# High and low weight halves behind the exponent and the scaled probabilities; unit 7's split a step sooner, one modulation piece a step later

## The reference, cut to what matters

```python
q, k, v, f, z = jnp.split(h @ w_in, SPLIT0, axis=-1)
...
logits = jnp.concatenate([sink_logits(sink, s_win.shape[:-1]), s_ctx, s_win], axis=-1)
p = jax.nn.softmax(logits, axis=-1)
...
y = jnp.concatenate([windowed_attention(q, k, v, kc, vc, sink), fourier_mix(f, w_f)], axis=-1)
x = x + gate[:, None] * ((y * jax.nn.silu(z)) @ w_out)
```

## Time and profile before

| | us |
|---|---|
| median of 3 runs | 1442.05 (1441.32 to 1442.59) |
| profiled execution | 1441.64 |
| its span, first to last instruction | 1440.0 |
| TensorE busy | 1409.8 |
| VectorE busy | 904.3 |
| ScalarE busy | 501.6 |

### The profile page before, as it was taken

The page is one execution under the profiler, slowest core; times in us unless marked ns, Lnnn a source line. Parts: engine busy times, 40 slices in busy tenths (PEclk is TensorE's granted clock), DMA queues, the critical chain, the costliest instruction groups (busy, mean ns, idle before and its releaser), DMA issues.

```text
span 1440.0 us, 20122 instructions
## 1 busy us (share of the span) xinstructions
PE 1409.8 (98%) x7714; PEld 1183.1 (82%) x7714; DVE 904.3 (63%) x1422; ACT 501.6 (35%) x730; POOL 77.1 (5%) x148
## 2 busy tenths in 40 slices
PE   5999999999999999999999999999999999999997
PEld 3788888888888888888888888888888888888897
DVE  6645656456767687776556676664555666674456
ACT  5223322244555344444222342112351323332233
POOL 0001111011100000000010001000000000010000
PEclk9999999999999999999999999999999999999999
DMA  9996667557611333324666656333323232366345
GB/s 384 408 385 223 197 214 255 165 177 217 206 58 54 105 109 115 117 75 158 204 193 191 199 177 205 117 91 100 99 92 102 88 101 90 98 197 191 104 145 174
DMA packets 65099, 236.87 MB, mean 164 GB/s; under 512 B 7232, under 2 KB 8128, under 8 KB 63744
## 3 DMA queue, kind: packets, MB, share of 16 engines
q1 hardware_dynamic: 43344, 157.83, 33.2%
q0 software_dynamic: 19712, 72.03, 16.0%
q10 hardware_dynamic: 1968, 5.95, 1.2%
HBM read 231.59 MB, written 4.19 MB: 164 GB/s over the span
## 4 chain that ended last, share of the span: by engine, by line
PE 93%; DVE 5%; issue 1%; ACT 1%; DMA 0%; DVEq 0%; ACTq 0%
PE ps L1385 91%; PE ps L1613 2%; DVE w_lo L798 1%; DVE kvmem L944 1%; DMA vec<-in_vectors 0%; DVE stat L1065 0%; DVE pooled L1346 0%; DVE kvmem L860 0%; DVE tmp L917 0%; DVE pt_lo L1104 0%; DVE modchunk L805 0%; DVE main L921 0%; DVE tmp L1076 0%; ACT scratch L533 0%; DVE h_lo L870 0%
## 5 line engine op out<-in xcount | busy, mean ns | idle before, releaser
L1385 PE MATMUL ps<-h_hi,w_hi 128*128 128x512 f32 (+1 forms) x1664 | 643.2, 387 | 1.0 <-DVE w_lo L798 0.5
L1385 PE MATMUL ps<-h_hi,w_lo 128*128 128x512 f32 (+1 forms) x1664 | 634.6, 381 | 0.0
L1385 PE MATMUL ps<-h_lo,w_hi 128*128 128x512 f32 (+1 forms) x1664 | 634.2, 381 | 0.0
L798 DVE TENSOR_TENSOR w_lo<-raw,w_hi 128x1024 fp32r<-128x1024 f32 x216 | 264.3, 1224 | 358.4 <-ACT w_hi L437 358.0
L437 ACT CAST w_hi<-raw 128x1024 fp32r<-128x1024 f32 x216 | 226.5, 1049 | 646.1 <-PE ps L1385 646.0
L1385 PEld LDWEIGHTS ps<-h_hi,w_hi 128*128 128x128 f32 x1664 | 312.9, 188 | 63.7 <-issue 5.4
L1385 PEld LDWEIGHTS ps<-h_hi,w_lo 128*128 128x128 f32 x1664 | 312.8, 188 | 61.2
L1385 PEld LDWEIGHTS ps<-h_lo,w_hi 128*128 128x128 f32 x1664 | 313.2, 188 | 56.8 <-issue 0.2
L805 DVE CUSTOM_DVE_ANT_0 modchunk<-modchunk,cond_row 128x1024 f32<-128x1024 f32 x128 | 154.8, 1219 | 21.1 <-DMA modchunk<-in_modb 21.1
L392 POOL DMA_DIRECT2D modchunk<-in_modb x128 | 67.6, 528 | 1140.2 <-DVE modacc L805 1115.8
L641 ACT CAST pt_hi<-ps 128x512 fp32r<-128x512 f32 (+1 forms) x48 | 30.7, 639 | 124.1 <-PE ps L1613 124.1
(11 more groups left out here) (206 smaller groups left out, 1343.5 us busy)
## 6 DMA issues: line engine op xcount, KB each, us to landing
raw<-in_weights SPq DMA_DIRECT2D x216, 512.0 KB, 3.6
modchunk<-in_modb POOLq DMA_DIRECT2D x128, 512.0 KB, 4.6
raw<-in_mod SPq DMA_DIRECT2D x32, 512.0 KB, 8.6
modchunk<-in_mod SPq DMA_DIRECT2D x16, 512.0 KB, 7.2
cond_row<-in_mod SPq DMA_DIRECT2D x16, 512.0 KB, 9.0
main<-in_xT SPq DMA_DIRECT2D x4, 1024.0 KB, 8.9
main<-in_xT ACTq DMA_DIRECT2D x4, 1024.0 KB, 4.9
out<-pooled SPq DMA_DIRECT2D x14, 256.0 KB, 2.1
```

The source lines that it names most:

```text
L798: nc.vector.tensor_tensor(w_lo[:, j % 2], src, w_hi[:, j % 2].bitcast(F32), ALU.subtract).then_inc(lo_ready, 1)
L1385: return nc.tensor.matmul(out, lhsT, rhs, start=start, stop=stop, skip_group_check=True)
```

## The change

Two tables change: the sixth entry of `UNIT_SLOTS` (the split of unit 7, counted from 0, the last of the group) from step 11 to 10, and the fifth of `JOB_SLOTS` from 10 to 11, where now two pieces stand. In a step, `hi` goes from the front of ScalarE's list to behind the exponent, and `lo` from behind the maximum to behind the scaled probabilities, ahead of modulation pieces, tile splits and rotations. In the first pass `hi` stands ahead of the swap. The work is the same.

```diff
-UNIT_SLOTS = (2, 4, 6, 7, 9, 11, 13)
+UNIT_SLOTS = (2, 4, 6, 7, 9, 10, 13)
 QUERY_SLOTS = (2, 5, 8)
-JOB_SLOTS = (1, 3, 5, 8, 10, 11, 12)
+JOB_SLOTS = (1, 3, 5, 8, 11, 11, 12)
...
-                    if k in UNIT_SLOTS:
-                        s = UNIT_SLOTS.index(k)
-                        hi(i + G_Z, s + 2)
                     if k in QUERY_SLOTS:
...
                     if k < STEPS and (k or first):
                         exponent(i, k)
+                    if k in UNIT_SLOTS:
+                        s = UNIT_SLOTS.index(k)
+                        hi(i + G_Z, s + 2)
...
-                    if k in UNIT_SLOTS:
-                        s = UNIT_SLOTS.index(k)
-                        if s < HALVES - 2 or last:
-                            lo(i + G_Z, s + 2)
                     if k in QUERY_SLOTS:
...
                     if k < STEPS and (k or first):
                         probabilities(i, k)
-                    if k in JOB_SLOTS and not (first or last):
-                        job(i + (M_Z - 1), JOB_SLOTS.index(k))
+                    if k in UNIT_SLOTS:
+                        s = UNIT_SLOTS.index(k)
+                        if s < HALVES - 2 or last:
+                            lo(i + G_Z, s + 2)
+                    for j, slot in enumerate(JOB_SLOTS):
+                        if slot == k and not (first or last):
+                            job(i + (M_Z - 1), j)
```

## The result

The changed kernel takes 1448.91 us, the median of 6 runs (1448.12 to 1450.13), against 1441.9 for the kernel before in the same comparison: 7.0 us more, a ratio of 1.0047 with a 95% interval of 1.0037 to 1.0058. The forecast was 1448.6 us. The profiled execution took 1448.12 us with a span of 1446.4, 6.4 above the span before; it is the shortest of the six.

The account below looks back on a forecast made before the run. TensorE was taken to bound the kernel, but VectorE the ends of passes two and three. Chunk waits 6.8, gains 0.35 and 0.4, loss 0.5 made +6.5 us on 1442.05: 1448.6 us, 8-in-10 range 1445.9 to 1452.0.

Parts of the forecast that it names:

- The bound and the place: End of passes two and three: VectorE, not TensorE, sets the time, with 0.05 us of slack.
- The chain to the late chunk: Passes two and three: late fifth piece delays the seventh chunk's load; seventh piece 3.4 us late each time, 6.8 us.
- L: Time from POOL's issue of the seventh chunk's load to its landing, taken as 4.3 us (3.9 to 5.6).
- Step 11 of the first pass: Probabilities come sooner for the transposes of step 12: gain 0.35 us (0 to 0.8).
- Step 3 of the third pass: Scores no longer held by a query piece behind the low half at step 2: gain 0.4 us.
- Step 11 of the second and third pass: Waits of 0.2 to 0.25 us for probabilities vanish, but gain nothing at the pass end.
- The last pass: Step 10 gets the low half ahead of the tile splits, delaying step 11's probabilities: loss 0.5 us (0 to 0.9).
- The fit of step 4: Unit split at step 4 is ready for step 5's first filler with 0.35 us to spare; costed at nothing.
- A: Rival at the ends of passes two and three: the chunk's load is hidden after all; 1441.5 us, chance 7%.
- B: Rival across the attention stage: transposes gain at every step, excess of about 4 us goes; 1438 us, chance 2%.
- C: Rival: units also come late, step 4's 0.35 us missing, and paired DMA takes 5 to 5.6 us; 1452 us, chance 12%.
- D: Rival at the seventh chunk: POOL can't prepare the load while VectorE works, 1.3 us later; 1451.2 us, chance 7%.

Follow-up runs that it names:

- piece_7_late: The full change with the seventh modulation piece moved from step 12 to step 13; 1442.58 us, ratio 0.9998 to the kernel before.
- split_parts: The full change except that the fifth modulation piece stays at step 10; 1443.61 us, ratio 1.0010 to the kernel before.

## Why the prediction was right, point by point

**The bound and the place.** That VectorE sets the time at the end of passes two and three held: the low half came 2.99 us later and TensorE's filler 2.99 us later. The rows that made the point were the earlier trace rows, three engines across one pass end. The first engine to feel the delay was another than I had named: TensorE waited for the output of the last block (line 1084) and not for the query piece; both are queued behind the seventh piece, so the amount is the same. So the sign that I had given, a wait of about 3 us for the low half, was seen in two parts: 2.0 us for the block's output and 0.3 and 1.0 for the low half.

**The chain to the late chunk.** Fifth piece forecast at 522.5, measured 522.53; issue forecast 524.4, measured 524.41; seventh piece forecast 528.7, measured 528.27. The step that failed is L, the landing: its size, not the chain. I took 4.3 us because another load follows at once. The landing of the load at 524.41:

```profile
DMA to landing us min/median/max: 3.8/3.8/3.8
```

The second load didn't slow the first here; it took longer itself, 4.6 us from its own issue at 525.56. The row of 4.3 us that I took as nearest shared its time with a load issued ahead of it: SP had issued a weight load in the kernel before at 522.28, and that one landed only 4.3 us later. In the changed kernel the weight load is issued at 520.18 and takes 3.5 us, so it has landed before 524.41. The 3.9 of a load alone was the row to take. That doesn't hold for every pair: at 299 and 310 us of the changed kernel, with a weight load in flight at the first issue, both loads of a pair took 5.1 to 5.5 us. The term was 6.8 us and should have been 6.0.

**What was missing.** The sum had no term for TensorE's clock. A wait of 2 us on TensorE wasn't over here when it ended: products behind it ran at 1.2 GHz for some microseconds. In the profiled run of the change that is 0.8 us, all at the fourth pass; at the third it is given back by step 2. With the measured sizes the sum is 6.0 + 0.8 - 0.4 - 0.5 + 0.2 = 6.1, for the 6.0 us of lag gained in the stage. The total came out close by luck: the clock's 0.8 us, which I had left out, stand for the 0.8 by which L was too large. The other runs of the change point the same way: the two longest, 1450.1 us, have a mean granted clock of 0.993, the profiled one of 1448.12 us has 0.995. The median is 0.8 us above the profiled run; that the clock makes this too is likely by these means, but not shown.

**The gains.** Step 11 of the first pass: forecast 0.35 us; the wait at the transposes of step 12 fell from 0.64 to 0.20, and over the pass 0.36 us were won. Step 3 of the third pass: forecast 0.4, measured 0.44 to 0.54; the query piece ends before TensorE needs it. Step 11 of the second and third pass: the 0.25 us were won there, and as forecast they gave nothing at the end of the second pass, since VectorE decides there.

**The losses.** The last pass: forecast 0.5 us, measured 0.2. The transposes of step 12 still wait, as the row of the changed kernel shows:

```profile
676.16 0.66 PE L1614 MATMUL ps<-kvmem,tmp 128*128 128x128 f32 x4 [0.27 <-DVE tmp L1076]
```

The maximum of step 11 came as late as forecast: at 673.69 against 666.49, 1.0 us beyond the lag of 6.2. But the scaling of the probabilities came only 0.2 us late beyond that lag (675.62 against 669.20), because the low half no longer stood between the two; I had put it at 0.5.

The fit of step 4, which I had costed at nothing with 0.35 us to spare: in the changed kernel's second pass the low half starts at 485.01 and the filler at 486.72, without a wait.

```profile
485.01 1.23 DVE L798 TENSOR_TENSOR w_lo<-raw,w_hi 128x1024 fp32r<-128x1024 f32 x1 [0.19 <-ACT w_hi L437]
...
486.72 0.47 PE L1386 MATMUL ps<-h_hi,w_hi 128*128 128x512 f32 x1
```

**The rivals.** A and B fall with the two waits for chunks. C falls on both counts: no waits for units at steps 3 to 9, and L was short. D falls with the landing of 3.8 us: POOL's issue at 524.41 stood beside VectorE's sixth piece, which reads two operands from SBUF (the chunk and the conditioning row), and the landing was among the shortest of the stage (3.7 to 4.8 us). Nor was the 3.9 us that I held against D the shortest of all: the chunk issued at 582.00 in the kernel before landed in 3.6. The rule of the Trainium skill on page "SBUF - State Buffer", section "Who interferes with whom", on which D rested, shows no effect here; whether POOL reads SBUF when it prepares a load isn't in any row.

The second part of the change, then, makes the whole loss and more (9.8 us alone). The first part, with or without unit 7's split at step 10, moves the time by 1.3 us or less. Put beside a piece at step 9 or, better, eight spread pieces, it is part of the fastest versions; how much of the 3.3 us it brings, and how much the spread pieces would bring with the old order, wasn't tried.

## What to carry to other kernels

Two buffers mean that the load for piece n+2 starts only when piece n is done: moving piece n later moves that load later, and the piece to check is the one two further on, with the full turn-round (here 1.9 us to the issue and 3.8 to the landing) counted from the moved one. An order of equal length on a saturated engine can still cost microseconds if it brings two users of the same buffer closer. Where a stall of TensorE can't be avoided, the products behind it may run slow, as they did here; a few products without use in the gap cost less in these traces (0.9 and 3.2 us won), while of the medians (1.6 and 2.5 us) the intervals overlap.

## What the runs showed of the hardware

Waits of 2.0 to 2.5 us on TensorE, in a stage where it was otherwise busy, were followed by a granted clock of 0.50 to 0.88 over windows of 4 us, and by 1.00 in the same windows when products without use filled the gap. Waits of 0.8 to 1.0 us alone (piece_7_late, split_parts) were followed by 1.00. The fall came right behind one wait of 2.02 us, but behind another of 2.00 only after 2.7 us more, with a wait of 1.01 between. The price wasn't proportional to the wait: 0.9 us in the full change, 3.2 us with the piece alone, whose wait at the scores was 0.4 to 0.5 us longer. What exactly sets when the clock falls and comes back these runs don't tell.
